# Output stage: activations split to f16 halves before they are turned, and turned by DMA transposes instead of on TensorE

## The reference

```
h = RMSNorm(x) ; p = h @ w_in
A = sliding-window attention, 8 query heads over 2 key heads, window 128, with sinks
B = retention, 4 heads of 128, chunks of 128 tokens, RMS norm per head
x = x + concat(silu(g_A) * A, silu(g_B) * B) @ w_out
```

## Time and profile before

| | |
|---|---|
| median of 3 runs | 2056.47 us (2053.58 to 2058.32) |
| profiled execution, its own time | 2057.81 us |
| its span, first to last instruction | 2055.3 us |
| TensorE busy | 1915.4 us, 93% |
| VectorE busy | 1451.5 us, 71% |
| ScalarE busy | 782.3 us, 38% |
| mean granted TensorE clock | 0.976 of full speed |
| stage O of layer 0, by TensorE's first and last matmul | 883.8 to 1093.3 us |
| stage O of layer 1, likewise | 1866.7 to 2050.9 us |

### The profile page before, as it was taken

One profiled execution on the slowest core, in us unless ns is written; L12 is line 12 of the kernel. 1 busy time (PEld: TensorE's weight loads), 2 busy tenths in 40 slices (PEclk: granted clock), 3 DMA queues, 4 the chain that ended last, 5 costly groups with the idle time before them and its releaser, 6 DMA issues.

```text
span 2055.3 us, 38859 instructions
## 1 busy us (share of the span) xinstructions
PE 1915.4 (93%) x12808; PEld 1111.9 (54%) x12808; DVE 1451.5 (71%) x5064; ACT 782.3 (38%) x1977; POOL 67.7 (3%) x108
## 2 busy tenths in 40 slices
PE   2279999999999999999998999999999999999999
PEld 2246565555555555554554655565555555555454
DVE  6548999987665676668874799999766567666342
ACT  5634555552222223234653445555322221223121
POOL 4000000010000000030001000000000000000000
PEclk9589999999999999999999999999999999999999
DMA  8631000021100210053333000001210021002442
GB/s 277 235 106 28 16 16 10 15 74 60 31 10 10 96 60 10 13 190 115 131 124 123 28 15 11 15 13 34 80 50 10 13 96 60 10 10 91 144 153 92
DMA packets 68283, 137.52 MB, mean 67 GB/s; under 512 B 9808, under 2 KB 40720, under 8 KB 67888
## 3 DMA queue, kind: packets, MB, share of 16 engines
q1 hardware_dynamic: 58464, 100.76, 14.3%
q0 software_dynamic: 9728, 35.66, 5.1%
HBM read 97.27 MB, written 49.68 MB: 71 GB/s over the span
## 4 chain that ended last, share of the span: by engine, by line
PE 40%; DVE 12%; issue 2%; ACT 2%; DMA 1%; DVEq 0%; SPq 0%; ACTq 0%
PE PA L461 16%; PE PB L461 15%; DVE r L997 2%; DVE r L973 1%; DVE mix L1037 1%; DVE w_mx L830 1%; PE OB L626 1%; PE S L607 1%; PE TK L596 1%; ACT r L1541 1%; PE S L642 1%; PE X L648 1%; PE OB L633 1%; PE X L559 1%; PE TK L648 1%
## 5 line engine op out<-in xcount | busy, mean ns | idle before, releaser
L461 PE MATMUL PA<-w_a,hT 128*128 128x512 f16 (+1 forms) x1920 | 403.1, 360 | 8.1 <-DVE land L951 8.1
L461 PE MATMUL PB<-w_a,hT 128*128 128x512 f16 (+1 forms) x1920 | 402.1, 359 | 0.0
L461 PEld LDWEIGHTS PA<-w_a,hT 128*128 (+1 forms) x1920 | 185.3, 99 | 181.3 <-DVE land L951 9.0
L461 PEld LDWEIGHTS PB<-w_a,hT 128*128 (+1 forms) x1920 | 184.6, 98 | 178.1 <-issue 10.5
L1541 ACT ACTIVATE r<-r,nm,unqk 128x256 f32<-128x256 f32 x256 | 150.5, 589 | 116.2 <-DVE sd L1005 116.2
L1599 ACT ACTIVATE r<-OB 128x128 f32<-128x128 f32 (+1 forms) x136 | 36.3, 272 | 386.5 <-PE S L642 360.1
L461 PE MATMUL PA<-w_b,hT 128*128 128x512 f16 x768 | 179.3, 384 | 0.0
L461 PE MATMUL PA<-w_b,r 128*128 128x512 f16 x768 | 177.1, 382 | 1.9 <-DVE r L1191 1.6
L461 PE MATMUL PB<-w_b,hT 128*128 128x512 f16 x768 | 176.3, 379 | 0.0
L461 PE MATMUL PB<-w_b,r 128*128 128x512 f16 x768 | 173.8, 379 | 0.0
L1086 DVE TENSOR_TENSOR r<-S,t_dec 128x256 f32<-128x256 f32 x64 | 27.1, 424 | 153.6 <-PE S L607 153.5
(11 more groups left out here) (239 smaller groups left out, 3036.1 us busy)
## 6 DMA issues: line engine op xcount, KB each, us to landing
out<-r SPq DMA_DIRECT2D x40, 512.0 KB, 2.6
r<-mixed SPq DMA_DIRECT2D x32, 512.0 KB, 4.5
r<-out SPq DMA_DIRECT2D x32, 512.0 KB, 3.5
r<-in_x_prompt SPq DMA_DIRECT2D x16, 512.0 KB, 6.1
w_b<-in_w_in POOLq DMA_DIRECT2D x16, 512.0 KB, 9.0
mixed<-mix SPq DMA_DIRECT2D x32, 256.0 KB, 2.0
w_a<-in_w_in POOLq DMA_DIRECT2D x16, 512.0 KB, 8.1
mixed<-mix SPq DMA_DIRECT2D x64, 128.0 KB, 1.8
```

The costliest lines, as they stand in the source:

```text
L461: last = nc.tensor.matmul(out[0:s.rows, 0:n], lhs, w16(ph, k, p, wpart), start=(k == 0 and part == 0 and wpart == 0), stop=(k == KT - 1 an ...
```

## The change

The rows are split into halves before they are turned, with the tokens still on the partitions. `o_mhi` (ScalarE) now writes f16(mixed * scale) straight from `mxt` into `mh`, and `o_mlo` (VectorE) writes the remainder with one instruction over 128x1024. SP then turns each half with a DMA transpose (`dma_start_transpose`) of 128x1024 f16 from `mh` to `mT` (`mixed_T`). The new x goes the same way in layer 0: `x_high`, `x_low`, and two transposes to `hT` (SP's new `h_T`). The functions `o_mscale`, `o_Tm` and the two-bank copies of the stage O are gone; the prologue keeps the old way. TensorE in the stage O has only its matmuls, and waits for `o_tm`, which the transposes raise when they land. VectorE's order changes too: `o_add` of piece 1 moves to the next step, `o_scale`, `o_mhi` and `o_mlo` work two steps ahead, and in the eight steps with weight chunks `w_low` 0 stands ahead of `h_rstd`, and `w_low` 1 and 2 stand together at the end.

```diff
+        mT = tuple(r2[:, o:o + 1024].bitcast(F16).rearrange("p (e n) -> p e n", e=2 * KT) for o in (2336, 1312))
+        mTs = r2[:, 0:256].bitcast(F16).rearrange("p (e n) -> p e n", e=2 * KT)
+        mh = tuple(r2[:, o:o + 1024].bitcast(F16).rearrange("p (e n) -> p e n", e=2) for o in (3360, 288))
+        xh = land[:, 1, 0:1024].bitcast(F16).rearrange("p (e n) -> p e n", e=2)
...
+        def mT_of(s):
+            if s.sample:
+                return mTs
+            return mT[s.par if s.fixed and s.c < SAMPLE_AT else 1 - s.par]
+        def mh_of(s):
+            return mh[0 if s.fixed and s.c < SAMPLE_AT else 1 - s.par]
+        def mt_count(L, s):
+            return 32 * (L * (9 - s.par) + s.half)
...
-                        pe.wait_ge(o_lo, L * STEPS + s.v + 1)
+                        pe.wait_ge(o_tm[s.par], mt_count(L, s) + 32)
                     if ph == "A" and p == 0:
-                        pe.wait_ge(h_lo, L * STEPS + s.v + 1)
+                        pe.wait_ge(h_lo, 32 * (L * STEPS + s.v + 1))
...
-            def o_Tm(L, s):
-                if s.fixed and s.c == SAMPLE_AT + 1:
-                    pe.wait_ge(o_lo, L * STEPS + s.v)
-                alone(pe, o_ms, L * STEPS + s.v + 1)
-                tr8(msc, m_banks(s), s.rows).then_inc(o_tm, 1)
...
-                    [lambda: b_ST("B1", L, F - 1), lambda: o_Tm(L, T0)],
+                    [lambda: b_ST("B1", L, F - 1)],
...
-                def o_work(s):
-                    return [[] if s.fixed and s.c == STEPS - 1 else [lambda: o_Tm(L, s + 1)], [], o_h(s - 1), []]
...
+                step2("O", L, T0, [[lambda: b_ST("B1", L, F)], [lambda: b_OS("B1", L, F)], [], []])
+                step2("O", L, T1, none)
                 proj_sample("O", L)
...
+                with pe.Fori(0, (STEPS - 3) // 2) as i:
+                    for c in (3, 4):
+                        step2("O", L, mid(c, i), none)
...
             def o_mlo(L, s):
-                m = mT[s.par]
-                lo(o_hi, 2 * (L * STEPS + s.v), m_banks(s), s.rows,
-                   lambda e, q: m[:, 4 * q:4 * q + 4, e, 0:s.rows]).then_inc(o_lo, 1)
-            def h_lo_part(L, s):
-                lo(h_hi, 2 * hn(L, s), h_banks(L, s), s.rows,
-                   lambda e, q: hT[:, e, 4 * q:4 * q + 4, hcols(s)]).then_inc(h_lo, 1)
+                r, b, m = s.rows, s.par, mh_of(s)
+                v.wait_ge(o_hi, L * STEPS + s.v + 1)
+                V.scalar_tensor_tensor(out=m[0:r, 1, :], in0=mxt[0:r, b, :], scalar=minv[0:r, b:b + 1],
+                                       in1=m[0:r, 0, :], op0=ALU.mult, op1=ALU.subtract).then_inc(o_lo, 1)
+            def x_low(L, s):
+                r, b = s.rows, s.par
+                v.wait_ge(x_hi, L * STEPS + s.v + 1)
+                V.scalar_tensor_tensor(out=xh[0:r, 1, :], in0=xt_[0:r, b, :], scalar=xy[0:r, b:b + 1],
+                                       in1=xh[0:r, 0, :], op0=ALU.mult, op1=ALU.subtract).then_inc(x_lo, 1)
...
+                def o_step(s, k=None):
+                    far = not (s.fixed and s.c >= STEPS - 2)
+                    if not (s - 1).sample:
+                        o_add(L, s - 1, 1)
+                    if not (s.fixed and s.c == 1):
+                        old = T0 if s.sample else T1 if s.fixed and s.c == SAMPLE_AT + 1 else s - 2
+                        v.wait_ge(dve_piece, piece("O", L, old, 1) + 2)
+                        o_unscale(L, s)
+                    if far:
+                        o_scale(L, s + 2)
+                    if s.sample:
+                        o_add(L, s, 0)
+                        o_add(L, s, 1)
+                    if k is not None:
+                        w_low(L + 1, "A", k, 0)
                     if not last:
                         h_rstd(L, s - 1)
-                    if not (s.fixed and s.c == STEPS - 1):
-                        v.wait_ge(dve_piece, piece("O", L, s - 1, 1) + 2)
-                        o_unscale(L, s + 1)
-                        o_mlo(L, s + 1)
-                    if k is not None:
-                        w_low(L + 1, "A", k, 0)
-                    if not (s.fixed and s.c >= STEPS - 2):
-                        o_scale(L, s + 2)
-                    o_add(L, s, 0)
+                    if far:
+                        o_mlo(L, s + 2)
+                    if not last:
+                        x_low(L, s - 1)
+                    if not s.sample:
+                        o_add(L, s, 0)
                     if k is not None:
                         w_low(L + 1, "A", k, 1)
-                    if not last:
-                        h_lo_part(L, s - 1)
-                    o_add(L, s, 1)
-                    if k is not None:
                         w_low(L + 1, "A", k, 2)
...
             def o_mhi(L, s):
-                act.wait_ge(o_tm, L * STEPS + s.v + 1)
-                m = mT[s.par]
-                hi(m_banks(s), s.rows, lambda q: m[:, 4 * q:4 * q + 4, 0, 0:s.rows], o_hi)
+                r, b = s.rows, s.par
+                act.wait_ge(o_sc, L * STEPS + s.v + 1)
+                if s.fixed and s.c == 1:
+                    act.wait_ge(o_tm[0], mt_count(L, s - 1) + 32)
+                elif not (s.fixed and s.c == 0):
+                    act.wait_ge(o_tm[b], mt_count(L, s))
+                A.activation(mh_of(s)[0:r, 0, :], mxt[0:r, b, :], ACT.Copy, scale=minv[0:r, b:b + 1]).then_inc(o_hi, 1)
...
+            def x_high(L, s):
+                r, b = s.rows, s.par
                 act.wait_ge(h_rs, hn(L, s) + 1)
-                A.activation(xn_of(L, s)[0:r, :], x, ACT.Copy, scale=xy[0:r, col:col + 1]).then_inc(h_xn, 1)
-            def h_hi_part(L, s):
-                act.wait_ge(h_t, hn(L, s) + 1)
-                hi(h_banks(L, s), s.rows, lambda q: hT[:, 0, 4 * q:4 * q + 4, hcols(s)], h_hi)
+                act.wait_ge(h_lo, 32 * hn(L, s))
+                A.activation(xh[0:r, 0, :], xt_[0:r, b, :], ACT.Copy, scale=xy[0:r, b:b + 1]).then_inc(x_hi, 1)
...
                 def o_step(s, k=None):
                     if not last:
                         h_squares(L, s - 1)
-                    if not (s.fixed and s.c == STEPS - 1):
-                        o_mhi(L, s + 1)
+                    if not (s.fixed and s.c >= STEPS - 2):
+                        o_mhi(L, s + 2)
                     if k is not None:
                         w_high(L + 1, "A", k, 0)
                     if not last:
-                        h_norm(L, s - 1)
-                    if not (s.fixed and s.c >= STEPS - 2):
-                        o_mscale(L, s + 2)
+                        x_high(L, s - 1)
                     if k is not None:
                         w_high(L + 1, "A", k, 1)
-                    if not last:
-                        h_hi_part(L, s - 1)
-                    if k is not None:
                         w_high(L + 1, "A", k, 2)
...
+                def mixed_T(s):
+                    if s.fixed and s.c == 1:
+                        alone(sp, b_o, bn("B1", L, F) + 1)
+                    elif not s.sample and not (s.fixed and s.c == 0):
+                        old = T0 if s.fixed and s.c == SAMPLE_AT + 1 else T1 if s.fixed and s.c == SAMPLE_AT + 2 else s - 2
+                        alone(sp, pe_piece, piece("O", L, old, 1) + 1)
+                    for e, ready in ((0, o_hi), (1, o_lo)):
+                        alone(sp, ready, L * STEPS + s.v + 1)
+                        sp.dma_start_transpose(mT_of(s)[:, e * KT:(e + 1) * KT, :], mh_of(s)[0:s.rows, e, :]
+                                               ).then_inc(o_tm[s.par], 16)
+                def h_T(s):
+                    for e, ready in ((0, x_hi), (1, x_lo)):
+                        alone(sp, ready, L * STEPS + s.v + 1)
+                        sp.dma_start_transpose(hT[:, e, :, hcols(s)], xh[0:s.rows, e, :]).then_inc(h_lo, 16)
...
-                        next_mixed(T0)
+                        mixed_T(T0)
+                        load_mixed(L, S)
                     store_mix(ph, L, F - 1)
                     if ph == "B1":
                         sp.wait_ge(b_qk, (L + 1) * 2 * STEPS)
                         load_x(L, T1, ys, ysm)
+                        mixed_T(T1)
+                        load_mixed(L, T2)
...
+                def store_y(s):
                     sp.wait_ge(dve_piece, piece("O", L, s, 1) + 2)
                     sp.dma_start(xs(s, ys, ysm), xt_[0:s.rows, s.par, :]).then_inc(y_out[s.par], 16)
-                    if loads:
-                        alone(sp, y_out[s.par], 16 * (L * (9 - s.par) + s.half + 1))
-                        if not last:
-                            sp.wait_ge(h_xn, hn(L, s) + 1)
-                        load_x(L, s + 2, ys, ysm)
-                for c in range(3):
+                    if not last:
+                        h_T(s)
+                def o_step(s):
+                    if not s.sample and not (s.fixed and s.c == STEPS - 1):
+                        mixed_T(s + 1)
```

(73 more changed lines are left out.)

177 lines of the change are left out of this document (59 added, 118 removed).

## The result

The changed kernel takes 2063.03 us (median of 8 runs, 2060.18 to 2071.36) beside 2054.56 us of the kernel before (8 runs): a ratio of 1.0043, 95% interval 1.0029 to 1.0056. The prediction said 2040.5 and faster. The time is inside its range and on the other side of zero; the range reached up here for the rival of slow transposes, not for the case held likeliest, which ended at 2050. The profiled execution took 2066.14 us, span 2064.2, mean granted clock 0.964.

What follows compares the result with a forecast made beforehand. TensorE was taken to bound the kernel, with VectorE bounding layer 0's weight-chunk steps after the change. Terms -14.5 + 2.5 - 2 + 0 - 2 = -16 us from 2057.8, less 1.3 for the median, gave 2040.5 us; range 2012 to 2110.

Steps and rivals of the forecast that it cites:

- the case held likeliest: VectorE bounds layer 0 and layer 1 runs clean: 2030 to 2050 us, chance 0.52.
- Layer 0, the front: Start of layer 0's stage O, to T2's last `o_add`: removed transposes offset by a longer chain, 0, range -6 to +6.
- Gain given back at the starts: Rival: pairs land in 12 us, T0 to T2 lose about 4 us each in either layer; 2052 to 2060, chance 0.09.
- The weight-chunk steps: Layer 0's eight steps with weight chunks: 13.2 us each, VectorE bound with two new waits; with the other steps, -2 us.
- VectorE keeps up: Rival: the two new waits in layer 0 don't arise, eight steps save 22 us more; 2018 us, chance 0.13.
- Layer 1: Stage O of layer 1: -14.5 us for 17 transpose sets off TensorE, +2.5 for T1's halves at the start.
- The boundary: Between layers: a shorter VectorE chain, `x_high` and `x_low`, cuts TensorE's wait of 5.49 us; -2 us.
- Transposes too slow: Rival: SP's queue in layer 0 can't turn four halves a tile in time; some 2240 us at 6 us a half, chance 0.26.

Runs made afterwards that it cites:

- the kernel with the two orders: Changed kernel with ScalarE's and VectorE's weight-chunk work reordered and T2's rows turned before T0's new x: 2037.11 us with GpSimd's load, 2028.63 with ScalarE's.
- plain copies: Changed kernel with the prompt tiles' halves copied by plain transfers of the same size instead of being turned: 2047.31 us, ratio 0.9961.
- Undoing the waits: Changed kernel with only ScalarE's and VectorE's order in the eight weight-chunk steps changed: 2041.23 us, ratio 0.9923.
- the two runs with both orders: Changed kernel with weight-chunk work reordered and T2's rows turned before T0's new x: GpSimd issuing the weight load, 2037.11 us; ScalarE issuing it, 2028.63 us.

## Why the prediction failed

**The step that failed** is "Layer 0, the front", put at 0 with a range of -6 to +6. It had T1's halves start near 891 and T1 near 901; T1's pair took 19.1 us from its first issue to its last landing, and T1 started at 911.71. It priced the queue by a plain load that took 8.76 us beside the weights and didn't ask what a transpose does to that traffic. Measured: +17.4 us from T0's start to T2's last `o_add`. Cutting the load out takes 18.0 us from this stretch and 16.2 from the time, so this is shown: it is the weights and the transposes hindering each other. The state stores, caught in the same queue with ScalarE and VectorE behind them, weren't in the prediction at all, and the chain runs through them. "Gain given back at the starts" was the rival of this kind, at 0.09 and with 4 us a tile. It named the place; its 12 us for the three tiles were 5 too few in layer 0 and too many in layer 1, and its sum doesn't come out: twelve us in each layer would outweigh the gain by some 5 us and not leave it near 0.

**Also shown**: it isn't the bytes alone (in the kernel with the two orders the same 5.2 MB from ScalarE left T1 waiting 5.60 and not 12.47 us), and not the order of starts (a later load moved the stall to mid(4)). Turning has the larger part, the number of pieces a smaller one, and 5 us of the front's loss stay with plain copies. The Trainium skill says, "DMA: Bandwidth & Descriptors", section "Issuing engines are not separate DMA queues", that DMAs from all engines run on the same 16 DMA engines and that issuing from several saves only the sequencer's time. Without DMA transposes these runs agree: the load took 23.7 us from GpSimd and 25.0 from ScalarE. Beside DMA transposes they disagree: 8.5 us between the same load from GpSimd and from ScalarE. The measurement decides.

**The weight-chunk steps** were right in mechanism and size: 13.58 us a tile against 13.2, both waits where they were put (2.20 us for 2, 1.25 for 1.2). VectorE's two instructions over 128x1024 take 1.28 us each (1.27 said). Undoing the waits gave 22 us, the prediction's own figure for "VectorE keeps up". That rival's time of 2018 still counted the front as free. In the changed kernel the eight steps are 0.4 us each longer than said, so the stretch gave +0.8 for -2.

**Layer 1** was right in sign, -7.0 for -12. The transposes are gone from TensorE, and its tiles are 10.36 us apart. T1's pair, priced at 2.5 us, cost nothing: issued at 1890.09, it had landed when TensorE came to T1 at 1895.03, 5 us later at most. The missing us are T2's, which the prediction did not look at in this layer: 3.80 of waiting and 2.5 of slow clock. SP's order explains most of it: with T2's rows first, the layer's stretch is 4.9 us shorter. So the term is -14.5 + 6.3 = -8.2, and about 1 us of the measured -7.0 isn't assigned.

**The boundary** gave -3.3 for -2. TensorE's wait for VectorE fell from 5.49 to 4.37 us, and the last set of transposes of the new x, 0.9 us on TensorE, is gone there. Where the other 1.3 came from was not traced.

**"Transposes too slow"** is false as a rule for the stage: 3.2 us to landing, and four of them fit in a tile of 10.37 us, 2.6 each. The estimate of 10.5 us a half, from the Trainium skill's "VectorE: DVE Perf Modes", section "The three transpose paths", is not borne out by that. The estimate of 1.0 us, from the 261 GB/s of the Trainium skill's "DMA: Bandwidth & Descriptors", section "Latency and other measured facts", is nearer to the engines' own time. In layer 1, where the engines' share rose from 0.39 to 0.70, a pair added 0.70 x 10.36 - 0.39 x 11.23 = 2.9 us of engine time a tile, 1.4 a half. Where GpSimd loads weights, though, it was true for the pairs that met the load.

**Open**: why GpSimd's load and a transpose slow each other down so far. The traces show the share, the rate and the packets, not what an engine does inside. Whether it is the kind of queue, its larger packets (5.24 MB in 1408 and not in 9600), or that ScalarE's issues are held back when the engines are full, no run separates. Spreading the load in slices between the pairs wasn't run.

## What to carry to other kernels

A transfer that moves work off a busy engine must be priced beside the traffic of each stretch it lands in, above all next to a bulk load, and so must everything queued behind it. When a step's order is rewritten, lay it out instruction by instruction for every pair of engines that hand work to each other: two such waits cost this change 22 us, and moving a few lines gave them back. Then ask for each load which queue issues it.

## What the runs showed of the hardware

- While one pair of 128x1024 DMA transposes met a load of 5.2 MB from GpSimd's queue, the engines moved 170 GB/s at a DMA share of 1.11, and the pair took 17.3 us; with the same load from ScalarE's queue, 290 GB/s at 1.19 and 10.5 us (the two runs with both orders). Without a load the pair took 4.1 us.
- GpSimd's queue cut the 5.24 MB into 1408 packets, ScalarE's into 9600. Without DMA transposes both loads took about as long: 23.7 and 25.0 us.
- SP's issue of one transpose takes 1.25 us (median), and two took 22.02 us while GpSimd's load ran.
- A 128x1024 half lands 3.2 us after its issue (median of the changed kernel; 2.3 at the least, 17.7 at the most).
- Two stores of 64 KB queued behind such a pair landed after 19.4 and 21.4 us; with the load cut, after 3.5 and 3.9.
- A load issued by ScalarE holds its sequencer, not only the queue: 24 issues ran from 884.8 to 906.9, and ScalarE stood idle for 15.55 us ahead of its next activation.
